# Output projections of two attention layers: one native fp32 unit and seven three-pass units, and the order of the next stage's low parts

## What is computed

```python
o = ...                                    # [512, 1024], all heads of layer a (or b)
x = x + o @ w_out                          # 1024 x 1024, "a_out" and "b_out": what is changed
h = rmsnorm(x, norm_ffn[layer])
a, b = jnp.split(h @ w_up, 2, axis=-1)     # "a_up", "b_up": the next stage
x = x + (silu(a) * b) @ w_down             # "a_down", "b_down"
```

## Time and profile before

| | |
|---|---|
| median of 3 runs | 3135.63 us (3129.99, 3135.63, 3136.77) |
| profiled execution | 3130.21 us |
| its span in the profile | 3128.4 us |
| TensorE busy | 2828.5 us, 90% of the span |
| VectorE / ScalarE / GpSimd busy | 1920.5 / 851.1 / 1143.5 us |
| mean granted TensorE clock | 0.981 of full |

### The profile page before, as it was taken

The page is one execution under the profiler, slowest core; times in us unless marked ns, Lnnn a source line. Parts: engine busy times, 40 slices in busy tenths (PEclk is TensorE's granted clock), DMA queues, the critical chain, the costliest instruction groups (busy, mean ns, idle before and its releaser), DMA issues.

```text
span 3128.4 us, 34369 instructions
## 1 busy us (share of the span) xinstructions
PE 2828.5 (90%) x11584; PEld 1752.2 (56%) x11584; DVE 1920.5 (61%) x5019; ACT 851.1 (27%) x1634; POOL 1143.5 (37%) x824
## 2 busy tenths in 40 slices
PE   8898999977777777899998989999999999999998
PEld 3345444422223322344457656887888777478876
DVE  8956777887888887877659854443032177254411
ACT  4731111111111111111113852221132177222222
POOL 5303333444434333433311322444444333144442
PEclk9999999999999999999999999999999999999999
DMA  3129999999999999999983112222222212122222
GB/s 128 48 94 374 420 419 414 402 422 420 422 421 421 421 417 363 402 420 416 417 325 96 49 59 75 95 99 89 99 88 88 94 60 71 47 88 98 99 93 73
DMA packets 128348, 715.28 MB, mean 229 GB/s; under 512 B 15750, under 2 KB 19990, under 8 KB 62375
## 3 DMA queue, kind: packets, MB, share of 16 engines
q0 software_dynamic: 74352, 543.06, 42.1%
q1 hardware_dynamic: 52792, 168.10, 15.6%
q10 hardware_dynamic: 1072, 2.47, 0.2%
HBM read 711.24 MB, written 2.34 MB: 228 GB/s over the span
## 4 chain that ended last, share of the span: by engine, by line
PE 59%; DMA 21%; DVE 10%; ACT 4%; issue 3%; POOL 2%; another core or an unknown queue 0%; SPq 0%; ACTq 0%; DVEq 0%; POOLq 0%
PE ps L511 29%; DMA arena<-in_peer_uv,arena 17%; PE ps L713 11%; PE ps L384 4%; DMA ring<-in_peer_uv,arena 3%; DVE arena L997 3%; PE ps L1813 2%; PE ps L1269 2%; PE ps L744 2%; PE ps L1285 2%; PE ps L1256 2%; PE ps L1874 2%; POOL arena L1059 2%; ACT arena L1307 1%; DMA n<-in_peer_uv,arena 1%
## 5 line engine op out<-in xcount | busy, mean ns | idle before, releaser
L713 PE MATMUL ps<-arena 128*128 128x512 f32 x1792 | 842.8, 615 | 149.3 <-DVE arena L1008 147.9
L1059 POOL DMA_INDIRECT arena<-in_peer_uv,arena x448 | 467.0, 1042 | 806.4 <-PE ps L713 658.9
L997 DVE CUSTOM_DVE_ANT_0 arena<-arena,sq 128x1024 f32<-128x1024 f32 x448 | 531.2, 1223 | 246.5 <-DMA arena<-in_peer_uv,arena 244.6
L713 PEld LDWEIGHTS ps<-arena 128*128 128x128 f32 x1792 | 337.1, 195 | 607.3 <-issue 348.2
L404 POOL TENSOR_TENSOR w_lo<-ring,w_hi 128x1024 fp32r<-128x1024 f32 (+1 forms) x156 | 413.5, 2651 | 652.4 <-ACT w_hi L417 652.4
L511 PE MATMUL ps<-n_lo,w_hi 128*128 128x512 f32 x992 | 387.9, 394 | 5.6 <-DVE n_lo L453 5.6
L511 PE MATMUL ps<-n_hi,w_hi 128*128 128x512 f32 x992 | 392.2, 395 | 0.4 <-issue 0.4
L511 PE MATMUL ps<-n_hi,w_lo 128*128 128x512 f32 x992 | 389.6, 393 | 0.0
L861 ACT ACTIVATE arena<-arena,tok_scale 128x2 f32<-128x2 f32 x256 | 75.7, 296 | 1057.7 <-DVE arena L997 1057.6
L417 ACT CAST w_hi<-ring 128x1024 fp32r<-128x1024 f32 (+1 forms) x156 | 173.8, 1114 | 668.2 <-PE ps L511 668.2
L535 DVE TENSOR_TENSOR h<-ps,h 128x512 f32<-128x512 f32 x32 | 22.1, 691 | 327.4 <-PE ps L511 219.7
(11 more groups left out here) (294 smaller groups left out, 3947.2 us busy)
## 6 DMA issues: line engine op xcount, KB each, us to landing
ring<-in_a_up SPq DMA_DIRECT2D x44, 512.0 KB, 3.2
ring<-in_b_up SPq DMA_DIRECT2D x44, 512.0 KB, 3.2
ring<-in_a_in SPq DMA_DIRECT2D x40, 512.0 KB, 6.9
ring<-in_w_q SPq DMA_DIRECT2D x32, 512.0 KB, 8.0
ring<-in_b_q SPq DMA_DIRECT2D x24, 512.0 KB, 3.3
ring<-in_a_down SPq DMA_DIRECT2D x16, 704.0 KB, 4.0
ring<-in_b_down SPq DMA_DIRECT2D x16, 704.0 KB, 4.1
ring<-in_w_in SPq DMA_DIRECT2D x16, 512.0 KB, 3.2
```

The lines of the kernel that those rows point to most:

```text
L713: mm = pe.matmul(bank(2 * (tt % 2) + q), diag[:, no % DIAGS, r, :], uvrow[p][r][:, D + 512 * q:D + 512 * q + 512], start=slot + r == 0, st ...
L997: ins = dve.tensor_tensor_reduce(out=u, in0=u, in1=ntok[:, tt, :], scale=1.0, scalar=0.0, op0=ALU.mult, op1=ALU.add, accum_out=dots[:, p, ...
L1059: pool.indirect_dma_start(uvrow[p][r], None, t["peer_uv"], bass.IndirectOffsetOnAxis(ap=expert_id[:, tt, slot + r:slot + r + 1], axis=0)). ...
```

## The change

The stages a_out and b_out join the list of split stages (SPLIT). Their unit 0 stays native on `attn`; units 1 to 7 become `split_unit` with `o_hi` and `o_lo`, new tensors for the high and low parts of `attn` in the free part of the arena. ScalarE (`early` in `feed_from`) casts the weights of units 1 and 2 and makes the eight `o_hi` tiles while unit 0 runs; later it casts unit u when unit u-2 is done, and handles the next stage's tile u-3 after that. GpSimd makes `w_lo` of units 1 to 7 (`out_rests`). VectorE first makes eight `o_lo` tiles (`out_lows`), and then, in the loop over tiles, the low part of the next stage's tile k-1 after the residual add of tile k; only tile 7's is left behind the loop. `n_lo` shares memory with `attn`, and `attn` is now read last by unit 0 and by `o_lo`. The loads by SyncE and all the other stages are as before.

```diff
-SPLIT = (("a_up", "a_ffn"), ("a_down", None), ("kv", "kv"), ("b_q", "b_mix"),
-         ("b_up", "b_ffn"), ("b_down", None))
+SPLIT = (("a_out", "a_o"), ("a_up", "a_ffn"), ("a_down", None), ("kv", "kv"), ("b_q", "b_mix"),
+         ("b_out", "b_o"), ("b_up", "b_ffn"), ("b_down", None))
+WHOLE_FIRST = ("a_out", "b_out")
...
+        o_hi, o_lo = (rounded(x, arena_at + 4 * (3 + y) * T, DK, T) for x, y in (("o_hi", 0), ("o_lo", DK)))
...
-            return (lambda: tiles(range(DK - 1)), lambda: tiles([DK - 1]), lambda: take_root(act, name))
+            def early():
+                if source not in WHOLE_FIRST:
+                    tiles(range(DK - 1))
+                    return
+                out_high(act, source, 1)
+                for k in range(DK):
+                    if k == 2:
+                        out_high(act, source, 2)
+                    act.wait_ge((LA if source == "a_out" else LB).o_drained, k + 1)
+                    act.copy(o_hi[:, k, :], attn[:, k, :]).then_inc(n_split_hi, 1)
+                for u in range(3, DK):
+                    out_high(act, source, u)
+                    tiles([u - 3])
+                tiles(range(DK - 3, DK - 1))
+
+            return (early, lambda: tiles([DK - 1]), lambda: take_root(act, name))
...
+        def out_project(pe, name, norm):
+
+            u0 = FIRST_UNIT[name]
+            wait_tile(pe, FIRST_TILE[name])
+            pe.wait_ge(w_landed[0], 16 * (u0 // RING + 1))
+            for k in range(DK):
+                mm = pe.matmul(bank(0), ring[:, 0, k * P:(k + 1) * P], attn[:, k, :], start=k == 0, stop=k == DK - 1)
+            mm.then_inc(unit_done, 1)
+            for u in range(1, DK):
+                split_unit(pe, name, u // RING, u % RING, o_hi, o_lo, first=norm if u == 1 else None)
+
+        def out_high(act, name, u):
+
+            u0, j = FIRST_UNIT[name], u % RING
+            act.wait_ge(w_landed[j], 16 * ((u0 + u) // RING + 1))
+            if u >= 3:
+                act.wait_ge(unit_done, u0 + u - 1)
+            act.copy(w_hi[:, u % 2, 0:DK * P], ring[:, j, 0:DK * P]).then_inc(split_hi, 1)
+
+        def out_rests(pool, name):
+
+            for u in range(1, DK):
+                pool.wait_ge(split_hi, split_units[name] + u + 1)
+                pool.tensor_tensor(w_lo[:, u % 2, 0:DK * P], ring[:, u % RING, 0:DK * P], w_hi[:, u % 2, 0:DK * P],
+                                   ALU.subtract).then_inc(split_lo, 1)
+
+        def out_lows(dve, norm):
+
+            for k in range(DK):
+                dve.wait_ge(n_split_hi, split_tiles[norm] + k + 1)
+                dve.tensor_tensor(o_lo[:, k, :], attn[:, k, :], o_hi[:, k, :], ALU.subtract).then_inc(n_split_lo, 1)
...
         def swiglu_dve(dve, step, l):
             x = "ab".index(l)
+            out_lows(dve, f"{l}_o")
             for k in range(DK):
                 add_residual(dve, f"{l}_out", [k])
                 if k >= 2:
                     add_square(dve, f"{l}_ffn", k - 1)
-            split_low(dve, f"{l}_ffn", 0)
+                if k >= 1:
+                    split_low(dve, f"{l}_ffn", k - 1)
             add_square(dve, f"{l}_ffn", DK - 1)
-            for k in range(1, DK):
-                split_low(dve, f"{l}_ffn", k)
+            split_low(dve, f"{l}_ffn", DK - 1)
             take_rstd(dve, step, f"{l}_ffn")
...
         def swiglu_pool(pool, l):
+            out_rests(pool, f"{l}_out")
             split_rests(pool, f"{l}_up")
...
-            stream(pe, "a_out", [attn[:, k, :] for k in range(DK)])
+            out_project(pe, "a_out", "a_o")
...
-            stream(pe, "b_out", [attn[:, k, :] for k in range(DK)])
+            out_project(pe, "b_out", "b_o")
```

More of the change, by code:

```diff
@@ L393, in program @@
         for name, norm in SPLIT:
-            split_units[name] = sum(u for x, u, _ in STREAM if x in split_units)
+            split_units[name] = sum(u - (x in WHOLE_FIRST) for x, u, _ in STREAM if x in split_units) - (name in WHOLE_FIRST)
             if norm:
```

## The result

The changed kernel took 3099.82 us in the median of four runs (3099.51 to 3100.35), the kernel before 3134.77 us: a ratio of 0.9888, 95% interval 0.9875 to 0.9901, or 35.0 us less. The profiled executions differ less: spans of 3128.4 and 3098.1 us, 30.3 us. A later session, five runs of the changed kernel beside the one before, gave 3103.50 against 3135.34 us, 0.9897 (0.9881 to 0.9912), 31.8 us. Forecast were 31.2 us less and 3104.4 us, in a range of 3097 to 3116.

The account below looks back on a forecast made before the run. Bound by TensorE's pace inside the projection and VectorE at the handover. Two layers of 9.6 us plus handovers of 6.3 and 5.7 us make 31.2 us off the 3135.6 us median: 3104.4 us, range 3097 to 3116.

Parts of the forecast that it names:

- Pace: In a_out and b_out, units 1 to 7 take 5.50 us each instead of 6.87, 9.6 us less a layer.
- Front: At the projection's start, casts, copies and `o_lo` subtractions stay hidden: 0 to 1 us a layer, taken as 0.
- the row of 3244 ns: Longest VectorE low part before the change, lying where GpSimd was subtracting; agrees with the two excluding each other.
- Units 3 to 7: In the projection, cast and GpSimd subtraction have 1.3 to 1.9 us of room in each unit and cost nothing.
- Handover: Tile 7's residual add to the up stage's unit 1 drain: 12.3 us, gaining 6.3 (layer a) and 5.7 us (b).
- kv's rows: Profile rows of the kv stage, where only tile 7's low part is left behind the loop: 12.65 us there.
- new wait on `w_lo`: Before the up stage's first matmul, TensorE waits about 0.4 us for GpSimd's low weights of unit 0.
- rival 1: Up-stage handover: VectorE's last low part waits for GpSimd, losing 2 to 8 us, 3106 to 3112; chance 0.08.
- The level: Saving carried over to the three-run median, 5.4 us above the profiled execution: 3104.4 us instead of 3099.0.

Follow-up runs that it names:

- doubled rests: Changed kernel with one more GpSimd subtraction of a unit's size, into unused memory, ahead of each of the 14 low weights: 3118.73 us, ratio 0.9938.
- the experiment: Changed kernel with ScalarE's cast of the next stage's unit 0 ahead of its work on tile 6: 3101.45 us, stretches 57.79 us in both layers.

## Why the prediction was right

**Pace.** Seven units at 1.37 us less each were forecast, 9.6 us. Measured: 6.87 to 5.44, 1.43 each, 10.0 us (9.95 on the chain). The sum had taken the up stage's 5.50 for the split pace; passes in the projection are 0.2267 us apart, as in the down stages, and in the up, kv and query stages 0.2288. That is 0.7 us in the two layers that the forecast lacked. Making the units native again gave 9.95 us of passes back: shown.

**Front.** ScalarE's eight copies take some 0.54 us each, within my 0.52 to 0.72. VectorE was held through both of GpSimd's subtractions (8.87 us for the eight `o_lo`, 6.68 with one of them moved away), as the row of 3244 ns warned. The last `o_lo` was done at 1864.4; its pass, the last of the eight that TensorE's timeline has from 1864.76 on, came near 1866.3. So the room was 1.9 us where I had worked out 0.2 at worst: counted from the end of the last attention tile the low parts were done after 10.4 us instead of 12.0 (those not held follow 0.6 us apart, where the sum had 0.74), and their last pass came after 12.3 instead of 12.2. The doubled rests showed that this room can be used up: unit 1 was then 3.0 us late.

**Units 3 to 7.** Room of 1.3 to 1.9 us forecast, none lost; one more subtraction moved the mean pace to 6.19. One reading was off without a cost: the square sum does not fit behind GpSimd's subtraction but meets it, and took 1.88 us instead of 0.68 four times in each layer (1890.81 in VectorE's timeline above); VectorE still stood idle 0.61 us before the next residual.

**Handover.** 12.3 us forecast by kv's rows, 12.23 and 12.24 measured. The gains of 6.41 and 5.77 us match 6.3 and 5.7. The new wait on `w_lo`, put at 0.4 us, shows in the trace as 0.13 us, called "issue", and is worth 0.36 by the experiment. Of the 6.41 us in layer a only 2.5 were TensorE's idle time before (2.15, 0.17 and 0.16 us); the larger part is passes and a sum of squares no longer slowed by the clock. The prediction named the clock but did not split the gain; kv's handover, which it used as the price, was free of both. The hold-off that rival 1 feared for the last low part did not come: it began at 1902.02, 0.37 us ahead of GpSimd's 1902.39, and in layer b by as much. That margin is thin. The first rival's mechanism is real (it held the `o_lo` and the low part at 1868.53), but there it is covered.

**What the sum lacked.** TensorE began 0.3 us sooner after the last attention tile in each layer (0.05 us after its end instead of 0.33), 0.6 us. Unit 0 is no longer inside a loop of TensorE's program, which I take for the cause without having tested it. With 0.7 us of pace and 0.2 of the handovers that makes the stretches' 32.65 against 31.2. And 1.6 us were given back by the clock in the end, which no row of before could tell.

**The level.** The sum against the profiled execution, 3099.0, came out at 3100.35; the one against the median, 3104.4, which I gave, was 4.6 us high. The sum took the 5.4 us between that median and the profiled execution for a part of the level, and the four runs after it lay at the profiled execution's level instead. The 5.4 us probably arose in the part ahead of the change, where the traces scatter; no trace of those slower executions shows it. In the later session the median after was 3103.5, so that 3104.4 and 3099.8 differ by no more than that scatter, and how near a single median came is luck. The difference of 35.0 us overstates the change by some 4: the two stretches less what the end gave back are 31.0 us, and the later session showed 31.8.

## What to carry to other kernels

A handover is best priced by another handover of the same kernel that already has the new order: kv's rows gave 12.3 us where 12.2 was measured. Where three passes on split operands replace native float32, run the first unit natively while the parts are being made, since waiting for them costs the wait and then the clock behind it. And judge a local change by the stretch between two of its own events: here it repeats to 0.04 us, while the part ahead of it scatters by 10.

## What I had not expected of the hardware

- A pass of 128 x 512 over fp32r operands has two paces at full clock, 0.2267 us (projections and down stages) and 0.2288 us (up, kv and query stages), the same in every trace. A shift of 64 bytes changes neither; the cause is open. In a_out of the changed kernel the passes with `o_hi` of the first split unit are still 0.229 us apart.
- How long the half clock lasts after the same wait of 6.2 us is not fixed: at b_down seven steps of 0.43 us before, eleven after, in the same code; over the eleven traces with that wait it is six or seven in four and eleven to thirteen in seven.
- The part ahead of the change puts the same point at 1850.3 to 1861.0 us, and most of that is there 70 us into the gather. Its cause is open too.
